# Attention of the sample tokens on four column groups of TensorE, a group's scores in one burst

## What is computed

```python
def diff_attn_sample(q, k_past, v_past, k_new, v_new, lam):
    # q, k_new, v_new: (8, 4, 8 heads, 128); k_past, v_past: (8, 256, 8 heads, 128)
    def probs(qi, kpi, kni):
        s_past = einsum('bqhd,bkhd->bhqk', qi, kpi) * scale
        s_new = where(causal, einsum('bqhd,bkhd->bhqk', qi, kni) * scale, NEG)
        return softmax(concatenate([s_past, s_new], -1), -1)
    p = probs(q1, kp1, kn1) - lam * probs(q2, kp2, kn2)
    return einsum('bhqk,bkhe->bqhe', p[..., :256], v_past) + einsum('bhqk,bkhe->bqhe', p[..., 256:], v_new)
```

## Time and profile before

| | before |
|---|---|
| median of 3 runs | 1471.41 us (1467.73 to 1471.97) |
| span of the profiled execution, first to last instruction | 1465.0 us |
| TensorE matmul busy | 1253.8 us, 86% |
| TensorE weight loads busy | 963.9 us, 66% |
| VectorE busy | 916.1 us, 63% |
| ScalarE busy | 698.6 us, 48% |
| GpSimd busy | 252.7 us, 17% |
| DMA, mean | 207 GB/s |

### The profile page before, as it was taken

How to read it: one execution, slowest core, us unless ns; L and a number is a source line. 1 busy time by engine, 2 the same in 40 slices (tenths; PEclk the granted TensorE clock), 3 DMA queues, 4 the chain that set the end, 5 groups by cost and what they waited for, 6 DMA issues and landing times.

```text
span 1465.0 us, 16900 instructions
## 1 busy us (share of the span) xinstructions
PE 1253.8 (86%) x5888; PEld 963.9 (66%) x5888; DVE 916.1 (63%) x1112; ACT 698.6 (48%) x748; POOL 252.7 (17%) x261
## 2 busy tenths in 40 slices
PE   5989994599999996299999999989937999999930
PEld 4766764478888885277776666657736788888820
DVE  4256357498888885832321444464675988888836
ACT  4233223277777775222112544432224777777721
POOL 2021020241111121410000000000302411112314
PEclk9999995699999998599999999969858999999975
DMA  9302047269999996732230133213462899999842
GB/s 341 122 29 93 1 173 285 84 224 359 374 372 372 376 368 214 296 116 92 89 116 1 59 116 115 78 48 118 187 238 83 302 376 373 369 375 371 299 181 77
DMA packets 142529, 302.56 MB, mean 207 GB/s; under 512 B 11888, under 2 KB 12048, under 8 KB 142352
## 3 DMA queue, kind: packets, MB, share of 16 engines
q1 hardware_dynamic: 123024, 250.23, 47.9%
q0 software_dynamic: 19168, 51.31, 9.8%
q10 hardware_dynamic: 288, 0.36, 0.1%
HBM read 288.36 MB, written 30.28 MB: 217 GB/s over the span
## 4 chain that ended last, share of the span: by engine, by line
PE 78%; DVE 13%; DMA 3%; ACT 3%; issue 2%; POOLq 0%; POOL 0%; SPq 0%; DVEq 0%; ACTq 0%
PE ps L1422 20%; PE ps L1424 20%; PE ps L1423 20%; PE ps L1657 3%; DVE wl L868 2%; PE ps L1720 2%; PE ps L1705 2%; PE ps L1581 2%; DVE x L1225 2%; PE ps L1467 2%; ACT wh L617 2%; PE ps L1674 1%; PE ps L1691 1%; DMA xg<-x_rows,gcur 1%; DMA yl<-y_rows 1%
## 5 line engine op out<-in xcount | busy, mean ns | idle before, releaser
L868 DVE TENSOR_TENSOR wl<-raw,wh 128x2048 fp32r<-128x2048 f32 x210 | 481.0, 2314 | 221.3 <-ACT wh L617 217.4
L617 ACT ACTIVATE wh<-raw 128x2048 fp32r<-128x2048 f32 x210 | 398.4, 1915 | 202.0 <-PE ps L1424 138.0
L1422 PE MATMUL ps<-wh,xTh 128*128 128x512 f32 (+1 forms) x560 | 227.7, 407 | 22.8 <-DVE wl L868 14.8
L1424 PE MATMUL ps<-wh,xTl 128*128 128x512 f32 (+1 forms) x560 | 223.0, 398 | 0.0
L1423 PE MATMUL ps<-wl,xTh 128*128 128x512 f32 (+1 forms) x560 | 223.0, 398 | 0.0
L1422 PE MATMUL ps<-wh,xgTh 128*128 128x512 f32 x512 | 209.3, 409 | 6.7 <-DVE xgTl L1175 5.7
L1423 PE MATMUL ps<-wl,xgTh 128*128 128x512 f32 x512 | 203.9, 398 | 0.0
L1424 PE MATMUL ps<-wh,xgTl 128*128 128x512 f32 x512 | 203.5, 398 | 0.0
L1422 PEld LDWEIGHTS ps<-wh,xTh 128*128 128x128 f32 (+1 forms) x560 | 98.6, 176 | 58.9 <-issue 22.5
L1422 PEld LDWEIGHTS ps<-wh,xgTh 128*128 128x128 f32 x512 | 97.3, 190 | 36.2 <-DVE wl L868 8.3
L1424 PEld LDWEIGHTS ps<-wh,xTl 128*128 128x128 f32 (+1 forms) x560 | 98.0, 175 | 34.2
(11 more groups left out here) (258 smaller groups left out, 1641.1 us busy)
## 6 DMA issues: line engine op xcount, KB each, us to landing
raw<-in_moe_w_up SPq DMA_DIRECT2D x120, 1024.0 KB, 10.5
raw<-in_moe_w_down SPq DMA_DIRECT2D x62, 1024.0 KB, 11.7
raw<-in_a_w_in SPq DMA_DIRECT2D x8, 1024.0 KB, 16.7
ahead_up<-in_moe_w_up SPq DMA_DIRECT2D x8, 1024.0 KB, 8.7
yl<-y_rows POOLq DMA_DIRECT2D x8, 1024.0 KB, 8.4
raw<-in_cache_k SPq DMA_DIRECT2D x16, 512.0 KB, 3.8
raw<-in_cache_v SPq DMA_DIRECT2D x16, 512.0 KB, 4.9
raw<-in_a_w_out SPq DMA_DIRECT2D x4, 1024.0 KB, 5.1
```

The costliest lines, as they stand in the source:

```text
L617: act.activation(wh[:, slot], src, ACT.Copy).then_inc(high[key], 1)
L868: dve.tensor_tensor(wl[:, slot], src, wh[:, slot].bitcast(F32), ALU.subtract).then_inc(low[key], 1)
L1422: pe.matmul(out, high_, w_high, start=start, stop=False)
L1424: return pe.matmul(out, low_, w_high, start=False, stop=stop)
```

## The change

The 128 columns of TensorE's array are used as four groups of 32. A matmul of 32 weight columns is placed on a group by `tile_position=(0, 32 * r)` and writes the 32 PSUM rows from `32 * r`.

**Scores.** Row `64 * b2 + 8 * h` lies in the group of rows `r = 2 * b2 + h // 4`. So only the 32 columns of `qpad` that belong to these rows are loaded, and the four groups take turns (`for i`, `for r`). All 16 matmuls of a group come in one burst at j = 5. What stood in `sample_scores` for the copied keys (`sm_ktc`) and for the slots (`keys_used`) is `keys_turned`, at j = 2 and 4. `sm_s` counts groups now, not sequences.

**Values.** Head `h` writes rows `32 * (h % 4)` and columns `128 * (h // 4)` of bank 6; bank 7 is not used. The copy to `o[4]` is four copies of 32x256, one a group of rows, and `sm_o` counts to 4.

```diff
@@ gpsimd, vector and tensor wait for four copies
-            pool.wait_ge(sm_o, 1)
+            pool.wait_ge(sm_o, 4)
...
@@ scalar
-                after(act, sm_s, 2 * (g - 1) + b2 + 1)
+                after(act, sm_s, g)
...
-            act.activation(o[4][0:NSAMP], ps[0:NSAMP, 6:8].rearrange("p a n -> p (a n)"), ACT.Copy).then_inc(sm_o, 1)
+            for r in range(4):
+                act.activation(o[4][0:NSAMP].rearrange("p (a r e) -> p a r e", r=4, e=P)[:, :, r],
+                               ps[NSAMP * r:NSAMP * (r + 1), 6, 0:2 * P].rearrange("p (a e) -> p a e", e=P),
+                               ACT.Copy).then_inc(sm_o, 1)
...
@@ vector: queries, sample_max
-                after(dve, sm_s, 2 * g)
+                after(dve, sm_s, g)
...
-                dve.wait_ge(sm_s, 2 * g + 2)
+                dve.wait_ge(sm_s, g + 1)
...
@@ tensor
-            def sample_scores(g, b2, half):
-
-                if half == 0:
-                    pe.wait_ge(sm_ktc, 8 * g + 4 * b2 + 4)
-                    pe.sem_inc(keys_used, 1)
-                    if b2 == 0:
-                        pe.wait_ge(new_keys, 2)
-                        pe.wait_ge(sm_q, g + 1)
-                        after(pe, sm_ptz, g)
-                for h in range(4 * half, 4 * half + 4):
-                    lhs = qpad[:, (b2 * 8 + h) * P:(b2 * 8 + h + 1) * P]
-                    mm = pe.matmul(ps[:, 5, 0:2 * P + NSAMP], lhs, kts[:, b2, h], start=(b2 == 0 and h == 0),
-                                   stop=(b2 == 1 and h == HEADS - 1), skip_group_check=True)
-                if half:
-                    mm.then_inc(sm_s, 1)
+            def keys_turned(g, b2):
+
+                pe.wait_ge(sm_ktc, 8 * g + 4 * b2 + 4)
+                pe.sem_inc(keys_used, 1)
+
+            def sample_scores(g):
+
+                pe.wait_ge(new_keys, 2)
+                pe.wait_ge(sm_q, g + 1)
+                after(pe, sm_ptz, g)
+                for i in range(4):
+                    for r in range(4):
+                        b2, h = r // 2, 4 * (r % 2) + i
+                        rows = slice(NSAMP * r, NSAMP * (r + 1))
+                        c0 = (b2 * 8 + h) * P + NSAMP * r
+                        mm = pe.matmul(ps[rows, 5, 0:2 * P + NSAMP], qpad[:, c0:c0 + NSAMP], kts[:, b2, h],
+                                       start=(i == 0), stop=(i == 3), skip_group_check=True,
+                                       tile_position=(0, NSAMP * r))
+                mm.then_inc(sm_s, 1)
...
@@ sample_values (the eight matmuls on ptn likewise)
-                    mm = pe.matmul(ps[0:NSAMP, 6 + h // 4, h % 4 * P:(h % 4 + 1) * P], ptz[:, page, b2, h],
+                    r = NSAMP * (h % 4)
+                    mm = pe.matmul(ps[r:r + NSAMP, 6, h // 4 * P:(h // 4 + 1) * P], ptz[:, page, b2, h],
...
-                                   skip_group_check=True)
+                                   skip_group_check=True, tile_position=(0, r))
...
@@ the loop
-                    if 2 <= j < 6:
-                        sample_scores(g, (j - 2) // 2, (j - 2) % 2)
+                    if j in (2, 4):
+                        keys_turned(g, j // 2 - 1)
+                    if j == 5:
+                        sample_scores(g)
```

More of the change, by code:

```diff
@@ L1400, in _ @@
             turn_low(T_O + 2, subg)
-            dve.wait_ge(sm_o, 1)
+            dve.wait_ge(sm_o, 4)
             squares(4)
@@ L1719, in sample_values @@
                 for h in range(HEADS):
-                    mm = pe.matmul(ps[0:NSAMP, 6 + h // 4, h % 4 * P:(h % 4 + 1) * P], ptz[:, page, b2, h],
+                    r = NSAMP * (h % 4)
+                    mm = pe.matmul(ps[r:r + NSAMP, 6, h // 4 * P:(h // 4 + 1) * P], ptz[:, page, b2, h],
                                    vals[:, page, h * P:(h + 1) * P],
-                                   start=(g == 0 and b2 == 0 and page == 0 and h % 4 == 0), stop=False,
-                                   skip_group_check=True)
+                                   start=(g == 0 and b2 == 0 and page == 0 and h < 4), stop=False,
+                                   skip_group_check=True, tile_position=(0, r))
                 if page:
@@ L1759, in _ @@
             for h in range(HEADS):
-                mm = pe.matmul(ps[0:NSAMP, 6 + h // 4, h % 4 * P:(h % 4 + 1) * P], ptn[:, h],
-                               x[0:NSAMP, 4, h * P:(h + 1) * P], start=False, stop=(h % 4 == 3), skip_group_check=True)
+                r = NSAMP * (h % 4)
+                mm = pe.matmul(ps[r:r + NSAMP, 6, h // 4 * P:(h // 4 + 1) * P], ptn[:, h],
+                               x[0:NSAMP, 4, h * P:(h + 1) * P], start=False, stop=(h >= 4), skip_group_check=True,
+                               tile_position=(0, r))
             mm.then_inc(sm_pv, 1)
-            pe.wait_ge(sm_o, 1)
+            pe.wait_ge(sm_o, 4)
             def turn_o(t):
```

## The result

The changed kernel takes 1433.34 us, median of four runs (1431.22 to 1436.23), against 1471.69 before (four runs); the ratio is 0.9746, interval 0.9716 to 0.9777. Faster was right; 1451 and the range from 1446 were not.

A forecast was written before the change was run, and what follows sets the result against it. TensorE was taken to bound the attention loop. Scores, values and tail, less form changes and squares, saved 18.8 to 23.6 us, taken as 20.5: span 1465.0 to 1444.5, plus 6.4 gives 1451; range 1446 to 1474.

The forecast's parts named there:

- What bounds the kernel: Attention loop: TensorE bounds it, and nothing hides the 1.94 us score burst of a step, so what is taken counts.
- Scores and values: Sample attention loop: score bursts save 3.2 to 3.7 us per group, twelve value bursts 0.53 to 0.77 us each.
- the first rival: Sample scores and values: four column groups work at once, saving 36 us, to 1435; chance 0.11.
- Loads: Score and value bursts: each new column group may show its 0.03 us weight load; sum 18.8 with loads open, 23.6 without.
- the third rival: Score and value bursts: groups run one after another with loads exposed, 6 to 22 us, to 1479; chance 0.09.
- the pairs of the prediction: Bursts: only a matmul's second pass overlaps the next one's first; score burst 4.1 to 4.6 us; clock up, chance 0.51.
- Form changes: Before each group's score burst: one more change of matmul form, 4 x 0.1 = 0.4 us lost.
- the burst in step 5, buffers and slots: Loop steps 2 to 7: gathering scores in step 5, with key buffer and cache slots freed as planned, costs nothing.
- The squares: Sums of squares on VectorE, steps 19, 21, 27 and 29: lost TensorE cover costs 2 us for all four.
- The tail: Behind the loop, last values and copies: net 3.3 us saved, taken as 2 because VectorE's weight-chunk split is late next.
- The fourth rival: Attention loop: pairs overlap but the clock falls inside the loop, costing about 9 us, to 1460; chance 0.15.
- Base: Whole kernel: counted from the 1465.0 us span, with the median 6.4 us above the span.

## Why the prediction was wrong, step by step

- **What bounds the kernel**: right. Nothing hid the bursts, and the second group of steps got shorter by just what its bursts did.
- **Scores and values**: the step that failed. It said that the second pass of a matmul, which must follow the first on its column group, holds up the matmul behind it on another group. The two passes do follow each other; they hold up nobody else, up to four passes a group. A burst is 8 lengths and not 17, 1.94 us (2.07 by the growth of its step) and not 4.1 to 4.6; a value burst about 4 and not 9. Over the loop that is 4 x 5.7 instead of 4 x 3.2 to 3.7, and 12 x 1.29 instead of 12 x 0.53 to 0.77: 38.3 instead of 19.2 to 24.0. The order was an assumption without a row; 1.94 us was named beside it as one end and priced as the first rival, to which I gave 0.11.
- **Loads**: 0.03 us of each new group was counted as possibly in the open. They are not: the 32 passes with their 32 loads fill 8.1 lengths.
- The rule of the Trainium skill that the third rival drew on (TensorE: Matmul & The Clock Gate, What overlaps and what doesn't) has loads overlap only for another row group, and matmuls start and end in program order. The trace does not agree between column groups: with four matmuls in a row on one group, the next group starts beside the fifth pass of eight, and 32 loads add nothing to eight pass lengths. The speed-up of 2.38 times that the same page of the Trainium skill gives for three tiles would have been nearer than the pairs of the prediction. Here 32 passes on four groups fill 8.1 lengths, 4.0 times; by the growth of the step it is 7.76/2.07 = 3.7.
- **Form changes, the burst in step 5, buffers and slots**: right or too small to see. A score burst starts 0.20 us behind the transposing pass ahead of it, as charged; no wait for keys or queries stands in front of a burst, and steps 6 and 7 kept 2.9 and 3.0 us.
- **The squares**: 2 us charged at the right steps. The wait itself was 1.88 us at step 20 (0.82 with the squares spread); with the fall of the clock behind it, steps 20 and 21 lost 5.8.
- **The tail**: 2 us, capped by VectorE's split. Measured 2.6 in the traces, and VectorE came last as said (953.03 to 955.31, low half at 955.23); four copies took 1.57 us where 1.5 was estimated.
- **The fourth rival**, the fall of the clock inside the loop, came true beside the first one: one fall ahead of the one that was there before, and 5.8 us with the wait in front of it, where 9 were priced.
- **Base**: the median was taken as 6.4 us above the span; the runs show 1.9, so the traced execution of before was 5 us under its median. Of the 17.7 us between 1451 and 1433.3, 11.9 lie between the spans (32.4 instead of 20.5), 4.5 are this, and about 1 is the changed kernel's median under its traced execution.

## What to carry to other kernels

Small fp32 matmuls of up to 32 weight columns are worth placing on four column groups, even though each is two passes: the cost is that of the longest group. Issue them so that no more than two matmuls stand in a row on one group; four in a row cost 20 lengths instead of 8. After such a gain, look at what the taken work had covered on other engines, and read the clock of the stretch behind every new hole before believing a gain in one stage.

## What was not expected of the hardware

- Each column group of 32 columns behaves like a queue of four passes (or two matmuls of two passes), one at work and three waiting, filled in program order: 8.1, 8.2, 12.2 and 20.3 pass lengths for four orders of the same 32 passes.
- Passes on different groups start within 0.02 us for four.
- A kernel of which 7 us were taken inside the loop came out 6 us slower in the median, with intervals that overlap. Four of its six runs took 1439 to 1442 us, with a mean clock of 0.900 to 0.904; but the changed kernel took 1433.8 us at 0.903, so the mean clock alone doesn't explain them.
